# Norms of a two-layer hybrid decoder: more of the token sums formed by TensorE

## What is computed

```python
def layer_norm(x, g, b):
    mu = jnp.mean(x, axis=-1, keepdims=True)
    var = jnp.mean(jnp.square(x - mu), axis=-1, keepdims=True)
    return (x - mu) * lax.rsqrt(var + LN_EPS) * g + b

x = layer_norm(ALPHA * x + 0.5 * swiglu(x, gate1, up1, down1), ln1_g, ln1_b)   # which = 0
p = x @ w_in                                    # latent attention, short convolution, S5, gates
x = layer_norm(ALPHA * x + mixed(p) @ w_o, ln2_g, ln2_b)                        # which = 1
x = layer_norm(ALPHA * x + 0.5 * swiglu(x, gate2, up2, down2), ln3_g, ln3_b)   # which = 2
```

## Time and profile before

| | us |
|---|---|
| median of 3 runs | 2515.97 (2514.27 to 2517.18) |
| the profiled execution | 2516.44 |
| its span, first to last instruction | 2514.5 |
| PE busy | 2482.0 |
| DVE busy | 1523.2 |
| POOL busy | 1343.0 |
| ACT busy | 1050.8 |
| chain that ended last | PE 90%, DVE 3% |

### The profile page before, as it was taken

The page is one execution under the profiler, slowest core; times in us unless marked ns, Lnnn a source line. Parts: engine busy times, 40 slices in busy tenths (PEclk is TensorE's granted clock), DMA queues, the critical chain, the costliest instruction groups (busy, mean ns, idle before and its releaser), DMA issues.

```text
span 2514.5 us, 50617 instructions
## 1 busy us (share of the span) xinstructions
PE 2482.0 (99%) x19900; PEld 2363.9 (94%) x19900; DVE 1523.2 (61%) x2678; ACT 1050.8 (42%) x1918; POOL 1343.0 (53%) x840
## 2 busy tenths in 40 slices
PE   9999999999999999999999999999999999999997
PEld 9999999998899999999999999999977788989897
DVE  7556956975453484535575569579844535935356
ACT  3555234235532243636345552342355322546363
POOL 4767435422244456858557674355222444769582
PEclk9999999999999999999999999999999999999998
DMA  5424323422233323333234243234322333334332
GB/s 146 135 68 109 89 77 95 111 79 68 59 80 89 101 77 101 102 101 102 83 90 135 68 106 92 77 94 112 82 65 58 87 94 97 85 101 119 86 104 79
DMA packets 479751, 232.61 MB, mean 93 GB/s; under 512 B 58960, under 2 KB 479056, under 8 KB 479536
## 3 DMA queue, kind: packets, MB, share of 16 engines
q1 hardware_dynamic: 460288, 220.53, 32.8%
q10 hardware_dynamic: 19248, 9.08, 1.5%
HBM read 220.79 MB, written 4.26 MB: 90 GB/s over the span
## 4 chain that ended last, share of the span: by engine, by line
PE 90%; DVE 3%; issue 2%; POOL 1%; ACT 1%; DMA 1%; ACTq 0%; POOLq 0%; DVEq 0%; SPq 0%
PE ps L749 54%; PE ps L894 24%; PE ps L869 3%; PE ps L781 2%; PE ps L1218 1%; POOL w_lo L670 1%; PE ps L1257 1%; PE ps L1222 1%; PE ps L1233 1%; ACT ln_in L1389 0%; ACT x_hi L1389 0%; PE ps L1140 0%; PE ps L1130 0%; DVE ln_in L1948 0%; PE ps L1235 0%
## 5 line engine op out<-in xcount | busy, mean ns | idle before, releaser
L670 POOL TENSOR_TENSOR w_lo<-w_raw,w_hi 128x1024 fp32r<-128x1024 f32 (+3 forms) x348 | 731.6, 2112 | 885.1 <-ACT w_hi L1389 884.8
L1389 ACT ACTIVATE w_hi<-w_raw 128x1024 fp32r<-128x1024 f32 (+3 forms) x348 | 315.6, 911 | 558.4 <-PE ps L749 248.7
L749 PE MATMUL ps<-x_hi,w_hi 128*128 128x264 f32 (+2 forms) x1904 | 290.0, 301 | 0.3 <-ACT w_hi L1389 0.2
L749 PE MATMUL ps<-x_hi,w_lo 128*128 128x264 f32 (+2 forms) x1904 | 280.4, 296 | 0.6 <-POOL w_lo L670 0.6
L749 PE MATMUL ps<-x_lo,w_hi 128*128 128x264 f32 (+2 forms) x1904 | 280.2, 296 | 0.0
L749 PEld LDWEIGHTS ps<-x_hi,w_hi 128*128 128x128 f32 x1904 | 253.7, 189 | 13.6 <-ACT w_hi L1389 0.7
L670 POOL TENSOR_TENSOR w_lo<-w_pair,w_hi 128x512 fp32r<-128x512 f32 x186 | 246.6, 1340 | 30.9 <-ACT w_hi L1389 30.9
L749 PEld LDWEIGHTS ps<-x_hi,w_lo 128*128 128x128 f32 x1904 | 252.4, 188 | 10.3 <-POOL w_lo L670 1.3
L749 PEld LDWEIGHTS ps<-x_lo,w_hi 128*128 128x128 f32 x1904 | 252.4, 188 | 9.1
L670 POOL TENSOR_TENSOR w_lo<-w_sum,w_hi 128x512 fp32r<-128x512 f32 x155 | 202.7, 1320 | 90.7 <-ACT w_hi L1389 89.1
L749 PE MATMUL ps<-hid_hi,w_hi 128*128 128x264 f32 (+1 forms) x1040 | 162.0, 300 | 0.5 <-DVE ln_in L1877 0.3
(11 more groups left out here) (350 smaller groups left out, 4904.2 us busy)
## 6 DMA issues: line engine op xcount, KB each, us to landing
w_raw<-in_w_in SPq DMA_DIRECT2D x82, 512.0 KB, 3.9
w_pair<-in_ffn_w_gate SPq DMA_DIRECT2D x64, 512.0 KB, 5.2
w_raw<-in_ffn_w_down SPq DMA_DIRECT2D x64, 512.0 KB, 4.1
w_pair<-in_ffn_w_up SPq DMA_DIRECT2D x60, 512.0 KB, 5.2
w_raw<-in_ffn_w_up SPq DMA_DIRECT2D x28, 512.0 KB, 3.8
w_raw<-in_ffn_w_gate SPq DMA_DIRECT2D x24, 512.0 KB, 3.8
w_raw<-in_ffn_w_down SPq DMA_DIRECT2D x32, 384.0 KB, 3.4
w_raw<-in_w_o SPq DMA_DIRECT2D x16, 512.0 KB, 3.8
```

The lines of the kernel that those rows point to most:

```text
L670: pool.tensor_tensor(held(w_lo, c), src, held(w_hi, c).bitcast(f32), ALU.subtract).then_inc(w_split, 1)
L749: ins = nc.tensor.matmul(dst, wk, x[:, k0 + k, tokens], start=first and k == 0 and n == 0, stop=last and k == n_tiles - 1 and n == 2)
L1389: return nc.scalar.activation(out, in_, f, **kw)
```

## The change

Only the first of the late tiles (`WHOLE` = 4) is still added on DVE. The sums over features of tiles 5, 6 and 7 and of their squares are formed by PE straight from z and from the square, accumulating in the same PSUM columns: for each half four sets of matmuls where there was one. In half 0 they stand in `last_tiles` (`around`), in half 1 in `first_products` (`between`), where the filler is gone and the first chunk takes its first three tiles (`LEAD`) ahead of the second chunk. Mean and variance become `token_stats`: that of half 0 ahead of tile 4's second half for nk = 8 and behind it for nk = 6; that of half 1 inside the tail of half 0. The takes of the second half move by `TAKES_IN`. ACT restores z for `which` = 1 too, and `turn_inputs` and `turn_step` wait for POOL's x_lo of half 1.

```diff
-FILLER = [(4, 8), (0, 7), (0, 10)]
+LEAD = 3
+SUMS_AT = 4
+TAKES_IN = {6: {1: 5, 2: 6, 3: 7}, 8: {1: 5, 3: 6, 5: 7}}
...
+        def square_row(k, h):
+            return 0 if k == KD - 1 and h is not None else 3 + k % 2
+        def restored(l, which):
+            return (2 * l + which - 1) * KD
...
             def norm(l, which, c0):
...
+                for n in range(SLOTS - 1):
+                    split(l, c0 + n)
                 root(l, which, 1)
+                split(l, c0 + SLOTS - 1)
...
+                turns = ([(k, j) for j in range(len(outs)) for k in range(lead)]
+                         + [(k, j) for k in range(lead, nk) for j in range(len(outs))])
+                for k, j in turns:
+                    out = outs[j]
+                    if (k, j) in between:
+                        between[k, j]()
...
             def first_products(l, c, x0, n):
                 sp = norm_span(n)
                 by_tiles(l, [pair(0, sp), pair(1, sp)], c, xh, xl, x_ready[0], x0, halves=(0,), sp=sp,
+                         free=[(z_half[1], n * 4 + (7 + j)) for j in range(2)], rests_last=n < 0,
+                         lead=LEAD if n >= 0 else 0,
+                         between={(0, 0): lambda: half_sums(n, 1, 4, 5), (0, 1): lambda: half_sums(n, 1, 6),
+                                  (SUMS_AT, 0): lambda: half_sums(n, 1, 7)} if n >= 0 else {})
+                if n >= 0:
+                    spread_mean(n, 1)
                 rounded(l, c + 2)
+                product(pair(2, sp), c + 2, 0, xh, xl, KD, True, True, split=(l, c + 2), halves=(0,), sp=sp,
+                        behind=[lambda: spread_root(n, 1)] if n >= 0 else [])
...
+            def token_sums(n, h, src, bank, first=True, last=True):
+                sp = norm_span(n)
+                for j in range(sp.blocks):
+                    t0 = sp.halves[h].start + j * sp.tok
+                    ins = nc.tensor.matmul(ps[0:sp.tok, bank, SUM_AT + j:SUM_AT + j + 1], src[:, t0:t0 + sp.tok],
+                                           ones[:, 0:1], start=first and j == 0, stop=last, skip_group_check=True)
+                return ins
+            def half_sums(n, h, *tiles):
+                for k in tiles:
+                    if k == WHOLE:
+                        pe.wait_ge(ln_sums, n * 3 + (h + 3))
+                        token_sums(n, h, stat[:, 1], 4 + h, True, False)
+                        token_sums(n, h, stat[:, 2], 6 + h, True, False)
+                        continue
+                    pe.wait_ge(z_half[h], n * 4 + (k - 3) + 4 * h)
+                    ins = token_sums(n, h, z[:, k], 4 + h, False, k == KD - 1)
+                    if k == KD - 1:
+                        ins.then_inc(ln_stat, 1)
+                    pe.wait_ge(ln_square, n * 12 + (k + 1 + 4 * h))
+                    ins = token_sums(n, h, stat[:, square_row(k, h)], 6 + h, False, k == KD - 1)
+                    if k == KD - 1:
+                        ins.then_inc(ln_stat, 1)
+            def around(n, d, p, nk):
+                at_ = (d - WHOLE) * 3 + p
+                if at_ == 0:
+                    half_sums(n, 0, 4, 5, 6)
+                if at_ == (1 if nk == KD else 2):
+                    half_sums(n, 0, 7)
+                if at_ == (2 if nk == KD else 3):
+                    spread_mean(n, 0)
+                if at_ == (3 if nk == KD else 5):
+                    spread_root(n, 0)
...
             def norm_out(l, which, k):
-                if which == 2:
+                if which:
...
             def layer_norm(l, which, bd, nk):
...
+                taken_in, rounded_in = TAKES_IN[nk], {6: (0, 2, 4), 8: (1, 3, 5)}[nk]
                 for k in range(KD):
                     norm_tile(l, which, k, 0)
                     if k:
                         norm_out(l, which, k - 1)
+                    if k in taken_in:
+                        square(l, which, taken_in[k], 1)
+                    if k in rounded_in:
+                        round_ahead(l, bd + 6 + rounded_in.index(k))
...
                 def take_half(k, h):
...
-                    total = ps[:, 4 + h, 0:sp.half]
-                    st.done(tt(total if k < KD - 1 else stat[:, 1, cols], total, z[:, k, cols], ADD))
+                    if k == WHOLE:
+                        st.done(tt(stat[:, 1, cols], ps[:, 4 + h, 0:sp.half], z[:, k, cols], ADD))
...
                 for k in range(WHOLE, KD):
-                    if k > WHOLE:
-                        st.done(add_half_square(k - 1, 0, k))
                     take_half(k, 0)
+                    if k == WHOLE + 1:
+                        add_half_square(0, 5)
+                if nk != KD:
+                    take_half(WHOLE, 1)
+                def token_stats(h):
...
-                    if h and which == 1:
-                        dve.wait_ge(x_ready[0], (n + 2) * KD)
-                        own = sp.halves[0]
-                        st.done(tt(z[:, :, own], xhf[:, :, own], xlf[:, :, own], ADD))
...
-                    if h == 0:
-                        st.done(add_half_square(4, 1, 9))
-                        take_half(5, 1)
...
-                                if which == 2:
-                                    dve.wait_ge(ln_out[0], l * KD + (k - 1))
+                                if which:
+                                    dve.wait_ge(ln_out[0], restored(l, which) + (k - 1))
                             stt(scaled(k), z[:, k, cols], par[:, col:col + 1], root, MUL, MUL).then_inc(ln_scaled, 1)
+                        if h == 0 and k == 0:
+                            add_half_square(1, 9)
...
-                        if h == 0 and k in (2, 3):
-                            st.done(add_half_square(k + 3, 1, k + 8))
-                            take_half(k + 4, 1)
-                        if h == 0 and k == 4:
-                            add_half_square(KD - 1, 1, 12).then_inc(ln_sums, 1)
+                        if h == 0 and k in TAKES_IN[nk]:
+                            take_half(TAKES_IN[nk][k], 1)
+                        if h == 0 and k == (7 if nk == KD else 6):
+                            token_stats(1)
+                token_stats(0)
+                if nk == KD:
+                    take_half(WHOLE, 1)
                 tail(0)
                 tail(1)
...
                 def turn_inputs():
                     if n >= 0:
-                        dve.wait_ge(ln_out[1], (n + 1) * KD)
+                        dve.wait_ge(x_ready[1], (n + 2) * KD)
...
                 ffn(l, 0, st)
+                dve.wait_ge(x_ready[1], l * 24 + 16)
                 for d in range(8):
                     turn_step(l, d, st)
```

More of the change, by code:

```diff
@@ L682, in norm @@
                 root(l, which, 0)
-                if l * 3 + which < 3 * DEPTH - 1:
-                    for n in range(SLOTS):
-                        split(l, c0 + n)
+                if l * 3 + which == 3 * DEPTH - 1:
+                    root(l, which, 1)
+                    return
+                for n in range(SLOTS - 1):
+                    split(l, c0 + n)
                 root(l, which, 1)
-                if l * 3 + which == 3 * DEPTH - 1:
-                    return
+                split(l, c0 + SLOTS - 1)
                 cols = norm_span(l * 3 + which).halves[1]
@@ L752, in product @@
                 return ins
[L754 to L785, removed]
@@ new lines, in by_tiles @@
+            def by_tiles(l, outs, c, hi, lo, ready, n0, nk=KD, halves=(0, 1), free=(), between={},
+                         sp=EVERY, rests_last=False, lead=0):
+                turns = ([(k, j) for j in range(len(outs)) for k in range(lead)]
[4 more added lines that the diff above has]
+                        between[k, j]()
+                    if k == 0:
+                        rounded(l, c + j)
+                        if j < len(free) and free[j]:
+                            pe.wait_ge(*free[j])
+                    if j == 0:
+                        pe.wait_ge(ready, n0 + (k + 1))
+                    for n, (w, x) in enumerate(((w_hi, hi), (w_hi, lo), (w_lo, hi))[:2 if rests_last else 3]):
+                        if k == 0 and n == 2:
+                            split_ready(l, c + j)
+                        for dst, tokens in columns(out, sp, halves):
+                            ins = nc.tensor.matmul(dst, held(w, c + j, k * P, (k + 1) * P),
+                                                   x[:, k, tokens],
+                                                   start=k == 0 and n == 0, stop=k == nk - 1 and n == 2)
+                    if k == nk - 1 and 1 in halves:
+                        ins.then_inc(chunk_done, 1)
@@ L865, in last_tiles @@
                                 split_ready(l, c + d)
-                            if p == 1 and h == 1 and d == WHOLE + 1:
-                                spread_mean(n, 0)
+                            if h == 1:
+                                around(n, d, p, nk)
                             for k in range(nk):
@@ L1942, in tail @@
```

(8 more changed lines are left out.)

60 lines of the change are left out of this document (16 added, 44 removed).

## The result

The changed kernel takes 2541.83 us (median of four, 2536.62 to 2548.41), the kernel before 2515.12 (median of four): 1.011 times as long (95% interval 1.0098 to 1.0122). The profiled execution took 2542.62 with a span of 2540.8. Slower, as forecast, but by 26.7 us where 13 were forecast, and outside the range.

What follows compares the result with a forecast made beforehand. PE, busy 2482.0 of 2514.5 us, was taken as the bound. Added sums and new waits, less lost waits and filler, gave +13.1; 2516.44 + 13.1 - .5 = 2529.0 us, range 2519 to 2538.

Steps and rivals of the forecast that it cites:

- the right rival: Clock falls in the norms where fillers stood; the 48 matmuls behind double, +5.8 a norm, in two norms 2541; 7%.
- wait (c): Norms 1, 2, 4: PE's second chunk waits for the take of tile 7's second half, .9, with refill 1.05.
- The work: Added sums on PE: 5.6 us in each norm of three blocks, 5.1 in norm 4, against 20.3 of waits and filler.
- t0: The start of the second half's first pass in `last_tiles`, from which the forecast counts times in each norm.
- Wait (a): Norms 0 and 3: DVE takes tile 4 of half 1 ahead of `token_stats(0)`, so PE waits 1.5 at `spread_mean`.
- Wait (b): Norms 0 and 3: tile 7's second half waits for the take of tile 5, moved behind the root: .5 more.
- PE's waits for POOL's x_lo: At the second `by_tiles` of norms 1, 2, 4; they go: -.6 in norm 2, -.3 each in norms 1 and 4.
- the last norm: Norm 5: the added sums follow without PE's earlier idle of 3.38; taken as -.5, bounds -1 and +.5.

Runs made afterwards that it cites:

- the second half's part alone: Changed kernel, but the first half's sums added on DVE and summed in one set as in the kernel before; second half by TensorE: 2518.43 us, ratio 1.0015.

## Why the prediction was half right

**The clock, the step that failed.** The forecast named the right rival (one-column matmuls and waits where fillers stood), gave it 7% and two norms, and measured it by idle time: 1.00 beside an idle of 1.02, .50 after 3.38, "my longest wait is 1.5". That criterion was wrong: in norms 1, 4 and 5 the clock fell with no idle of PE in the profile, behind one-column matmuls. It happened in five norms of six, and 16.4 us of span lie between the changed kernel and its twin with sums of 32 columns. That the rival's 2541 lies beside the measured 2541.83 is luck: it priced two norms, on top of a wait (c) that did not come.

The trace of before had a warning that was not read. The forecast says of PE's waits that no other is above 2.0 in total; the second row of that list is an idle of 2.6 that the profile puts down to no other engine. Its longer part lies in the S5 part, and behind it, though it is only half as long as the 3.38, the clock was at .50 from 520.6 to 524.0:

```profile
PE ps L1140 <- issue: 2.6, 2, 1.9
```

```profile
520.24 0.45 PE L1140 MATMUL ps<-s_state,s_out 64*64 64x66 f32 x11 [1.87 <-issue]
```

The Trainium skill (TensorE: Matmul & The Clock Gate, section on HAM oscillation) tells of waits between bursts of matmuls that send the clock back to its low level. The trace of before agrees at 520 and 2501; the changed kernel goes further, since in norms 1, 4 and 5 the clock fell without a gap in the profile.

**The work.** Three sets behind t0 took 2.77 (forecast 2.67 and a splice), later ones .89. Norm 2, which has no wait and no fall, grew by .65, where 5.6 of work less 5.2 makes .4. Right, some .2 to .5 a norm short: a run of six behind a run on another operand takes .47 (377.70 to 378.17), not .445.

**Wait (a)**: 1.34 twice (forecast 1.5). Right. **Wait (b)**: with 32 columns some .27 in norm 0 ahead of tile 7's second half (forecast .5). Under the slow clock it was nothing in norm 0, where PE came too late to wait, and .2 in norm 3. **Wait (c)**: none. This term was mis-sized, by 3.3 us in three norms. In norm 2 of the changed kernel DVE took tile 7 at 1278.91, done 19.7 behind t0 (1259.64), where 20.7 was forecast; PE came at 1279.59, 19.95 behind it:

```profile
1278.10 0.50 DVE L1990 SCALAR_TENSOR_TENSOR ps<-ln_in,par,ps 128x264 f32<-128x264 f32 x1 [0.62 <-ACT ln_in L1419]
...
1278.91 0.43 DVE L1923 SCALAR_TENSOR_TENSOR ln_in<-ps,ln_in 128x264 f32<-128x264 f32 x1
```

DVE's waits for ACT were .31, .62, .31, .62 up to there, 1.9 and not 2.5, and its steps follow each other closer: the twenty that end with this take took 8.5, not 9.1.

**x_lo and the rest.** PE's waits for POOL's x_lo are gone, as forecast. From one norm's spread to the next norm's t0, with 32 columns against before: -.1 behind norm 1 (forecast -.3), -.9 behind norm 2 (-.6), +.1 behind norm 4 (-.3), and +.2 from norm 5's t0 to the end (-.5): the last norm gained nothing.

Together: the forecast without the clock was +13.1, 2529.0. The kernel with sums of 32 columns, whose clock is nearly held, measured 2526.3, +11.9 over the kernel before on its chip, in the forecast's range. In part that is errors that cancel. In the table norms 1, 2 and 4 are 2.5 below the forecast (no (c), less the work that was short), and norm 3 is 1.7 above by its slow stretch. Between norms 0 and 1, where the forecast expected nothing, its trace is 3.6 shorter than that of before; this is no gain of the change, but the idle of 1.87 and the 3.4 us at .50 shown above, which stand in the trace of before and in no other (the idle there is at most 1.4 elsewhere, without a fall). The sum of work and waits was sound to within these; the branch with the larger price had the small chance.

## What to carry to other kernels

Where reductions over partitions go to TensorE as matmuls with one moving column, look at the granted clock of the trace around them, not at PE's busy share, which here stayed at 100% while the pace halved. Before reordering, try the same instructions with more columns: here that was free and gave back 15.5 us. And a work estimate that holds at one clock needs a second line, each stretch at .50 adding half its length, with a chance read from every place in the trace where the clock falls.

## What was not expected of the hardware

- A matmul with 88 (or 128) stationary columns takes the same time with 32 moving columns as with one: .89 for twelve, .81 for eight in norm 4.
- The clock fell to .50 with PE busy throughout by the profile, or behind a one-column run of only 1.8 us and the first .45 us of another, with an idle of .84 three passes earlier (the second half's part alone, norm 0), yet in norm 2 of one profile of the changed kernel a longer run left it at 1.00. From which run on it falls stays open.
- Nothing here tells why the stretches at .50 differ in length, 3.4 to 10.2 us, between norms with the same order of work.
